# Last stage of a two-block kernel: row sums added up on VectorE, C rows multiplied as high and low parts, first half's last norm placed beside the second half's products

## The reference, cut to what matters

```python
u = ca * jax.nn.sigmoid(cg)
u = depthwise_conv(u, lp['c_conv'], C_CONV // 2, C_CONV // 2)      # 31 taps, 512 channels
u = layer_norm_2(u, lp['c_ln_g'], lp['c_ln_b'])                    # mean and variance over 512 channels
yc = jnp.einsum('btc,ce->bte', jax.nn.silu(u), lp['c_pw']) + lp['c_pw_b']
...
cat = jnp.concatenate([ya * jax.nn.silu(za), yb * jax.nn.silu(zb),
                       yc * jax.nn.silu(zc), yd * jax.nn.silu(zd)], axis=-1)   # 4 x 512 rows
y = jnp.einsum('bte,ed->btd', cat, lp['w_out'])
x = x + gate * y
return rms_norm_2(x, final_g)                                      # over 1024 channels
```

## Time and profile before

| | us |
|---|---|
| median of 3 runs | 3508.3 (3506.18 to 3508.97) |
| profiled execution, its own time | 3508.35 |
| its span in the trace | 3506.2 |
| TensorE busy in the span | 3327.1 (95%) |
| VectorE busy | 1903.7 (54%) |
| ScalarE busy | 1057.7 (30%) |

### The profile page before, as it was taken

The page is one execution under the profiler, slowest core; times in us unless marked ns, Lnnn a source line. Parts: engine busy times, 40 slices in busy tenths (PEclk is TensorE's granted clock), DMA queues, the critical chain, the costliest instruction groups (busy, mean ns, idle before and its releaser), DMA issues.

```text
span 3506.2 us, 37170 instructions
## 1 busy us (share of the span) xinstructions
PE 3327.1 (95%) x15356; PEld 2669.9 (76%) x15356; DVE 1903.7 (54%) x3141; ACT 1057.7 (30%) x1537; POOL 146.6 (4%) x72
## 2 busy tenths in 40 slices
PE   8999999999999999999999999999899899888997
PEld 7888888777888877777778888888676677667675
DVE  4323323267768688785543223223766877876443
ACT  3121121224332556562321111111543331322321
POOL 0000000000000000000000000000001033060000
PEclk9999999999999999999999999999999999999998
DMA  4211211112533420014111111111112111103131
GB/s 149 75 56 60 72 61 53 68 61 96 133 117 113 163 84 13 13 48 163 37 37 49 54 43 49 54 48 49 60 37 96 64 37 64 64 24 108 54 144 48
DMA packets 86808, 246.96 MB, mean 70 GB/s; under 512 B 8304, under 2 KB 22000, under 8 KB 85104
## 3 DMA queue, kind: packets, MB, share of 16 engines
q1 hardware_dynamic: 86640, 244.58, 20.2%
HBM read 200.51 MB, written 44.04 MB: 70 GB/s over the span
## 4 chain that ended last, share of the span: by engine, by line
PE 78%; DVE 15%; ACT 5%; issue 1%; DMA 1%; DVEq 0%; SPq 0%; ACTq 0%
PE PS L359 77%; DVE CV L1823 2%; PE PS L364 2%; DVE X L1823 1%; DVE WS L1815 1%; DVE XC L1823 1%; DVE HELD L1858 1%; DMA RAW<-in_W 1%; DVE XS L1823 1%; DVE RG L1823 1%; DVE GG L1815 1%; ACT RG L1045 1%; ACT WS L1045 1%; ACT PT L1045 1%; DVE TMP L1823 1%
## 5 line engine op out<-in xcount | busy, mean ns | idle before, releaser
L359 PE MATMUL PS<-XS,WS 128*128 128x512 f32 x8352 | 1964.1, 396 | 75.8 <-DVE TMP L1815 24.6
L359 PEld LDWEIGHTS PS<-XS,WS 128*128 128x128 f32 x8352 | 1584.1, 190 | 440.7 <-issue 90.4
L359 PE MATMUL PS<-HS,WS 128*128 128x512 f32 x2208 | 511.3, 392 | 8.7 <-DVE WS L1815 8.7
L359 PEld LDWEIGHTS PS<-HS,WS 128*128 128x128 f32 x2208 | 416.2, 189 | 98.7 <-issue 12.0
L1045 ACT ACTIVATE WS<-RAW 128x1024 fp32r<-128x1024 f32 x280 | 286.5, 1050 | 532.1 <-PE PS L359 428.8
L1815 DVE TENSOR_TENSOR TMP<-TMP,PS 128x512 f32<-128x512 f32 x112 | 76.5, 686 | 653.5 <-PE PS L359 645.1
L1815 DVE TENSOR_TENSOR WS<-RAW,WS 128x1024 fp32r<-128x1024 f32 x280 | 339.1, 1233 | 166.5 <-ACT WS L1045 166.1
L1045 ACT ACTIVATE TMP<-PS 128x512 f32<-128x512 f32 x184 | 108.9, 596 | 542.6 <-PE PS L359 475.5
L1823 DVE SCALAR_TENSOR_TENSOR X<-PS,X 128x512 f32<-128x512 f32 x160 | 110.1, 690 | 240.9 <-PE PS L359 240.4
L1045 ACT ACTIVATE HS<-TMP 128x512 fp32r<-128x512 f32 x88 | 55.6, 632 | 478.5 <-DVE TMP L1815 478.5
L1823 DVE SCALAR_TENSOR_TENSOR CV<-UU,COL,CV 128x1024 f32<-128x1024 f32 x120 | 163.6, 1363 | 3.6
(11 more groups left out here) (282 smaller groups left out, 3011.8 us busy)
## 6 DMA issues: line engine op xcount, KB each, us to landing
RAW<-in_W SPq DMA_DIRECT2D x286, 512.0 KB, 3.7
DC<-TMP SPq DMA_DIRECT2D x32, 256.0 KB, 4.2
X<-in_xT SPq DMA_DIRECT2D x8, 512.0 KB, 8.5
DX<-X SPq DMA_DIRECT2D x2, 2048.0 KB, 8.1
DCZ<-CA SPq DMA_DIRECT2D x8, 512.0 KB, 4.0
DGA<-TMP SPq DMA_DIRECT2D x16, 256.0 KB, 2.7
DGB<-TMP SPq DMA_DIRECT2D x16, 256.0 KB, 3.8
CZ<-DCZ SPq DMA_DIRECT2D x8, 512.0 KB, 6.1
```

The source lines that it names most:

```text
L359: done = d.matmul(out, l, r, start=first, stop=last)
```

## The change

All of it is in the last stage, apart from six additions on VectorE in the mixer stage ahead of it.

- **Row sums.** Where TensorE summed a row block at a time (four matmuls for a mean or a sum of squares over 512 channels, eight over 1024), VectorE now adds the blocks in `HELD` or `TMP` first and TensorE makes one matmul of the sum (two for the very last one, whose eighth block comes directly). The sum of the `CV` blocks is built in the mixer, behind each channel block's convolution.
- **Order of `c_norm`.** Both means stand behind P1; the sum of squares of half 0 behind P3 and of half 1 behind P5. On ScalarE the squares of half 0 stand in the first piece and those of half 1 in the fourth, ahead of half 0's root and SiLU.
- **C rows.** The two `c_pw` units become split units (the plan's kind changes from raw to split). ScalarE copies the normed rows to `CVH`, VectorE writes the rest to `CVL`, and `cp` takes 12 fp32r matmuls where it took 4 plain ones. SP loads one unit more ahead of the stores of the C rows.
- **Last norm.** The squares of half 0 are summed as its blocks finish; TensorE's sum stands behind the second product of half 1, and root, reciprocal and scalings of half 0 stand among VectorE's additions for half 1. The output leaves in eight DMAs of 2 blocks instead of four of 4.

```diff
@@ tensor, c_norm and outputs
             def mean(h):
...
-                e.wait_ge(ve("ones"), ve("cv", 3), *banks.free(use))
-                mms(group(bank(*use), [(ones[:], CV[:, k, half(h)]) for k in range(4)])).then_inc(*mm.inc(*use))
-
-            mean(0)
-            yield
-            square_sum("c", 0, 4, lambda k: tmp("sq", "c", 0, k))
-            mean(1)
-            yield
-            yield
-            square_sum("c", 1, 4, lambda k: tmp("sq", "c", 1, k))
-            yield
-            yield
+                e.wait_ge(ve("ones"), ve("cvs", 3, h), *banks.free(use))
+                mms([(bank(*use), ones[:], HELD[:, h, :], True, True)]).then_inc(*mm.inc(*use))
+
+            def squared(h):
+                use = ("sq", "c", h)
+                banks.take(use, (ve, "v", "c", h))
+                e.wait_ge(ve("cq", h, 3), *banks.free(use))
+                mms([(bank(*use), ones[:], tmp("sq", "c", h, 0), True, True)]).then_inc(*mm.inc("sq", "c", h, 3))
+
+            for h in range(2):
+                mean(h)
+            yield
+            for h in range(2):
+                yield
+                squared(h)
+                yield
...
-                        mms(group(bank(*use), [(raw(u, 512 * (m % 2) + 128 * k, 128), CV[:, k, half(h)])
-                                               for k in range(4)])).then_inc(*mm.inc(*use))
+                        product(u, 512 * (m % 2), 4, CVH, CVL, h, use, ac("csh", 1, 3), ve("csl", 1, 3))
...
-                    if h == 1:
-                        square(0, m)
-                        if m:
-                            square(1, m - 1)
-            square(1, 7)
+                    if h == 1 and m == 1:
+                        row_squares(0)
+            row_squares(1)
+
+        def row_squares(h):
+
+            use = ("sq", "out", h)
+            banks.take(use, (ve, "v", "out", h))
+            e.wait_ge(ve("sqs", 6 + (h == 0), h), *banks.free(use))
+            done = mms([(bank(*use), ones[:], HELD[:, h, :], True, h == 0)])
+            if h:
+                e.wait_ge(ac("sq", "out", 1, 7))
+                done = mms([(bank(*use), ones[:], tmp("sq", "out", 1, 7), False, True)])
+            done.then_inc(*mm.inc("sq", "out", h, 7))
@@ scalar, c_norm
+            def squared(h):
+                for k in range(4):
+                    use = ("sq", "c", h, k)
+                    tmps.take(use, (ve, "cq", h, k) if k else (mm, "sq", "c", h, 3))
+                    e.wait_ge(ve("cc", h, k), *tmps.free(use))
+                    act(tmp(*use), CV[:, k, half(h)], ACT.Square).then_inc(*ac.inc(*use))
+            def scaled(h):
                 root("c", h)
                 for k in range(4):
+                    x = CV[:, k, half(h)]
                     e.wait_ge(ve("cy", h, k))
-                    x = CV[:, k, half(h)]
                     act(x, x, ACT.Silu, bias=col("c_ln_b", k)).then_inc(*ac.inc("cs", h, k))
...
+                for k in range(4):
+                    e.wait_ge(ac("cs", h, k), ve("xs", "ab", 5, 0))
+                    act(CVH[:, k, half(h)], CV[:, k, half(h)], ACT.Copy).then_inc(*ac.inc("csh", h, k))
+
+            squared(0)
+            for _ in range(3):
+                yield
+            squared(1)
+            scaled(0)
+            for _ in range(2):
+                yield
+            scaled(1)
             yield
@@ scalar, outputs
             for m in range(8):
                 square(0, m)
-                if m:
-                    square(1, m - 1)
-            root("out", 0)
-            square(1, 7)
+            for m in range(8):
+                square(1, m)
+                if m == 2:
+                    root("out", 0)
             root("out", 1)
@@ vector, mixer and c_norm
                 convolve(31)
+                if ct:
+                    for h in range(2):
+                        s = HELD[:, h, :]
+                        e.wait_ge(ve("cv", ct), ve("cvs", ct - 1, h) if ct > 1 else ve("ln4", "y0", 7, h))
+                        tt(s, s if ct > 1 else CV[:, 0, half(h)], CV[:, ct, half(h)], ALU.add).then_inc(*ve.inc("cvs", ct, h))
...
+            def split(h):
+                for k in range(4):
+                    e.wait_ge(ac("csh", h, k))
+                    low(CVL[:, k, half(h)], CV[:, k, half(h)], CVH[:, k, half(h)]).then_inc(*ve.inc("csl", h, k))
+
+            for h in range(2):
+                mean(h)
+            yield
+            for h in range(2):
+                center(h)
+            yield
+            for h in range(2):
+                sum_squares(h)
+                yield
+                scale(h)
+                yield
+            for h in range(2):
+                split(h)
+                yield
@@ vector, outputs
+            for m in range(8):
+                gated_add(("co", m, 1))
+                add_square(1, m - 1)
+                if m == 2:
+                    rstd("out", 0, 1024, RMS_EPS, mm("sq", "out", 0, 7), HELD[:, 0, :])
+                if 2 < m < 7:
+                    for k in (2 * m - 6, 2 * m - 5):
+                        scale_out(0, k)
+            rstd("out", 1, 1024, RMS_EPS, mm("sq", "out", 1, 7), HELD[:, 1, :])
+            for k in range(8):
+                scale_out(1, k)
@@ sync
+        loads(277)
         for m in range(4):
             for h in range(2):
                 store_cat(8 + m, h, ve("cp", m, h))
             if m % 2:
-                loads(276 + m // 2)
+                loads(278 + m // 2)
@@ pack
-    w += [(np.concatenate([cpw[2 * j], cpw[2 * j + 1]], axis=1), "raw") for j in range(2)]
+    w += [(np.concatenate([cpw[2 * j], cpw[2 * j + 1]], axis=1), "split") for j in range(2)]
```

More of the change, by code:

```diff
@@ L242, in build @@
     CV = at("CV", 152, [128, 4, 1024], F32)
+    CVH, CVL = at("CVH", 168, [128, 4, 1024], F32R), at("CVL", 152, [128, 4, 1024], F32R)
     PB = at("PB", 168, [128, 1026], F32)
@@ L999, in outputs @@
             for h in range(2):
-                if h == 1:
-                    banks.resize(6)
                 for m in range(8):
@@ L1771, in square @@
                 use = ("sq", "out", h, k)
-                tmps.take(use, (mm, *use))
+                tmps.take(use, (mm, "sq", "out", 1, 7) if h and k == 7 else (ve, "sqs", max(k, 1), h))
                 e.wait_ge(ve("co", k, h), *tmps.free(use))
@@ L2781, in c_norm, with mean, center @@
         def c_norm():
-            def c_mean(h):
-                e.wait_ge(mm("cm", h), ve("ln4", "y0", 7, h))
+            def mean(h):
+                e.wait_ge(mm("cm", h))
                 ts(HELD[:, h, :], bank("cm", h), 1.0 / 512, None, ALU.mult).then_inc(*ve.inc("cm", h))
-            def c_center(h):
+            def center(h):
                 for k in range(4):
@@ L2790, in c_center, with sum_squares, scale @@
                     tt(x, x, HELD[:, h, :], ALU.subtract).then_inc(*ve.inc("cc", h, k))
-            def c_scale(h):
+            def sum_squares(h):
+                s = tmp("sq", "c", h, 0)
+                for k in range(1, 4):
+                    e.wait_ge(ac("sq", "c", h, 0), ac("sq", "c", h, k), *([ve("cq", h, k - 1)] if k > 1 else ()))
+                    tt(s, s, tmp("sq", "c", h, k), ALU.add).then_inc(*ve.inc("cq", h, k))
+            def scale(h):
                 e.wait_ge(ve("cc", h, 3))
@@ L2859, in outputs, with add_square, scale_out @@
                         low(XS[:, 1, k, :], XSf[:, 1, k, :], XS[:, 0, k, :]).then_inc(*ve.inc("cr", k))
-            for h in range(2):
-                for m in range(8):
-                    gated_add(("co", m, h))
-            for h in range(2):
-                e.wait_ge(ve("cy", h, 3))
-                rstd("out", h, 1024, RMS_EPS, mm("sq", "out", h, 7), HELD[:, h, :])
-                for k in range(8):
-                    x = X[:, k, half(h)]
-                    e.wait_ge(ve("rs", "out", h))
-                    stt(x, x, col("final_g", k), HELD[:, h, :], ALU.mult, ALU.mult).then_inc(*ve.inc("fin", k, h))
+            def add_square(h, k):
+                s, x = HELD[:, h, :], tmp("sq", "out", h, k)
+                if k == 1:
+                    e.wait_ge(ve("cy", h, 3), ac("sq", "out", h, 0), ac("sq", "out", h, 1))
+                    tt(s, tmp("sq", "out", h, 0), x, ALU.add).then_inc(*ve.inc("sqs", 1, h))
+                elif k > 1:
+                    e.wait_ge(ac("sq", "out", h, k), ve("sqs", k - 1, h))
+                    tt(s, s, x, ALU.add).then_inc(*ve.inc("sqs", k, h))
+            def scale_out(h, k):
+                x = X[:, k, half(h)]
+                e.wait_ge(ve("rs", "out", h), ac("sq", "out", h, k))
+                stt(x, x, col("final_g", k), HELD[:, h, :], ALU.mult, ALU.mult).then_inc(*ve.inc("fin", k, h))
+            for m in range(8):
+                gated_add(("co", m, 0))
+                add_square(0, m - 1)
+            add_square(0, 7)
+            for m in range(8):
+                gated_add(("co", m, 1))
[8 more added lines that the diff above has]
+                scale_out(1, k)
```

(6 more changed lines are left out.)

27 lines of the change are left out of this document (removed).

## The result

| | us |
|---|---|
| before, median of 4 runs beside it | 3508.03 (3506.18 to 3508.97) |
| with the change, median of 4 runs | 3488.89 (3485.69 to 3490.11) |
| ratio, with its 95% interval | 0.9941 (0.993 to 0.9953) |
| profiled execution: own time, span | 3490.11, 3487.2 |

A forecast was written before the change was run, and what follows sets the result against it. TensorE was taken as the bound from P1 to half 1's last product. Terms 0.2 - 5.7 - 10.6 - 3.8 = -19.9 on the 3506.2 us span gave 3486.3, with time outside the span 3488.4; range 3480 to 3494.

The forecast's parts named there:

- Mixer, 0: Mixer stage: six additions behind the convolutions fit in VectorE's idle time and cost 0.
- Start of the stage, +1.2: Last stage's start: splitting the first `c_pw` unit ahead of A and B rows delays 1.2 us, counted within `c_norm`.
- `c_norm`, +0.2: C norm: twelve matmuls go, but ScalarE's and VectorE's chain eats the gain; `cp` starts 0.2 us later in all.
- `cp`, -5.7: C rows' product: eight products take 2.72 us each instead of 3.43, 5.7 us less.
- Half 0 and `do`, 0: From `cp` to the end of half 0: later splits are ready in time and additions fit, 0.
- Half 1, -10.6: Half 1's products: 22.6 us from half 0's last pickup instead of 33.27, 10.6 us less.
- tail, -3.8: Last product to the end: 3.8 us less than 25.95, with VectorE late and two sums at half clock.
- (2): Rival in `c_norm`: TensorE keeps the pace, the chain being 6 to 9 us shorter; 3479 us, chance 0.12.
- (3): Rival in `c_norm`: the chain is longer through half clock, about 5 us more; 3493 us, chance 0.12.
- (4): Rival on ScalarE: each table switch on the path costs another 1.4 us; 3491.2 us, chance 0.05.
- (5): Rival at `do`: the D rows' load comes late; slower, 3512 us if 38 us later; chance 0.02.
- (6): Rival on the whole kernel: less than 7 us won; chance 0.02.

The follow-up runs named there:

- experiment 1: The kernel before with only the last norm's part of the change, C norm and C rows as before; 3494.15 us, ratio 0.9956.
- experiment 8: The changed kernel with reordered C norm, earlier last-norm root, scalings moved into the wait, and first `c_pw` unit split behind the A and B rows; 3472.89 us.
- experiment 5: The changed kernel with C norm sums of squares in `HELD` and the C norm's steps in another order, same work; 3478.93 us, ratio 0.9914.
- experiment 2: The changed kernel with the C rows' product as plain float32 again, no high and low parts; 3490.74 us, ratio 0.9944.
- experiment 4: The changed kernel with half 0's sum, root and reciprocal of the last norm one product earlier; 3484.53 us, ratio 0.9931.
- experiment 6: The changed kernel with half 0's last-norm root one product earlier and its last four scalings behind the last addition of squares; 3483.07 us.
- experiment 7: The changed kernel with 18 fp32r matmuls of unused result ahead of the last two sums; 3488.68 us, ratio 0.9942.
- experiment 3: The changed kernel with the C norm's squares added into `HELD` instead of a `TMP` slot; 3486.37 us, ratio 0.9933.

## Why the prediction was right

Where a time of the changed kernel is set against a forecast one or one of before, the 0.92 by which its stage began late is taken off; other times are as the profile has them.

- **Mixer, 0.** The six additions cost nothing that can be seen. The start of the stage moved by 0.92, of which 0.45 was there at the 56th microsecond of the program, ahead of anything that was changed. Over the stretch with the additions (before 2773.71 to 3189.73) it was 416.0 us before, 416.4 with the change, and 416.3 in experiment 1, which has no additions there.
- **Start of the stage, +1.2.** Measured 1.14 (wait for `XS` 4.12 against 2.98); experiment 8 removed it.
- **`c_norm`, +0.2.** `cp` starts 0.18 later than before (first pickups less one product: 3313.61 - 2.72 = 3310.89 against 3314.14 - 3.43 = 3310.71). The chain, step by step, forecast against measured: sum of half 0 picked up 3273.3, 3273.3; table load done 3276.4, 3276.3; SiLUs done 3284.0, 3283.9; high parts done 3286.4, 3285.95; additions done 3290.6, 3290.2; wait 6.4, 6.1; low parts done 3310.9, 3310.4. The price of the high parts was off: I took it from four squares in 2.44, and they took 2.17. But those squares were paced by VectorE's centring, 2.49 for four, and three squares with nothing in their way take 1.68 in the changed kernel (3274.26). So I had read a wait as a price. The step that was off most is P6 to P8, priced 16.3 + 2 to end at 3310.6: TensorE needed 19.16 us from the start of the sum to the end of P8 where I had 20.0, and ended at 3309.4. It did not show, since the low parts set the start of `cp`. They were done 0.5 early, and what made up for that is 0.14 from their end to `cp`'s first matmul, and the time between a product's end and its pickup, which the sum left out. So the mechanism was right, and that +0.2 came out to the tenth is luck. That the gain of twelve plain matmuls is eaten by this chain is what experiment 5 shows: with the chain reordered, all 9.3 appeared.
- **`cp`, -5.7.** Pickups at 3314.53 and 3317.25 are 2.72 apart, before 3.43. The size was right; experiment 2 shows that its net worth is 0.9, since the splits delay P1 and lengthen the `c_norm` chain. The forecast had both halves of this in different terms and did not set one against the other.
- **Half 0 and `do`, 0.** The last pickup of half 0 (3442.37) is 5.53 earlier than before where 5.5 was forecast. The D rows' high parts began at 3356.35, `do` at 3376.9: 20 us ahead.
- **Half 1, -10.6, and tail, -3.8.** The last product ended 16.2 earlier, where 16.1 was forecast. The tail is 22.2 us (forecast 22.15): reciprocal of half 0 done at 3457.26 (3457.3), last addition of squares 3468.78 (3469.1), sums 3472.6 (3472.55), last scaling 3482.8 (3482.7), end 3486.3 (3486.3). Times in brackets are the forecast's. Experiments 4, 6 and 7 show each of its two parts, the wait and the clock.

**The rivals.** TensorE did not keep the pace (2): 6.1 us of wait. The chain was not longer (3): the granted clock was 0.84 in the two us from 3294 on, 3 us into the work. No table load cost more (4): 3275.95 + 1.28 = 3277.23, and the root starts at 3277.24. The Trainium skill (ScalarE: Activation LUTs, What ACT_TABLE_LOAD costs) gives a drain of about 1380 ns for each switch. The trace does not show it: the load starts 0.01 us behind the last square and the root 0.01 behind the load. The D rows were not late (5). The gain was not below 7 us (6).

The remaining 0.9 between the forecast span of 3486.3 and the measured 3487.2 is the later start of this execution's stage, scatter that no term had. Outside the span this execution had 2.9 us where 2.15 was assumed. By the trace each term of the sum is right to 0.1 us, and each step on the chain of `c_norm` to half a microsecond, while P8, which was off the chain, ended 1.2 ahead of its forecast; the median's agreement within 0.5 is finer than the scatter of 4.4 us between its own runs allows one to claim.

## What to carry to other kernels

When work is taken off the engine that is the bound, follow the other engines in their new order before counting the gain: here the matmuls taken out of `c_norm` and `cp` were won only where the chain of square, sum, root, reciprocal, SiLU and split kept up, and 9.3 us came back by ordering that chain alone. Look at what stands between two steps of such a chain for another purpose (a weight unit's copy, scalings that nobody waits for, a slot whose release is a sum on another engine) and move it into a wait that is there anyway. And judge a change of a few microseconds by the length of its stage in the trace: the start of the stage wandered by 3.4 us between executions of kernels that are the same up to there.

## What was unexpected of the hardware

- **The price of a wait on TensorE is more than the wait.** The last two sums, two plain matmuls, took 3.81 us to the pickup behind a wait of 4.75, and 2.02 behind one of 0.67. In experiment 4 I expected that behind a wait of 2 the clock would be up; the wait was 3.29, and the first sum still took 1.67 and the second 1.91 us, at a granted clock of 0.50. Behind 1.44 they took 1.13 and 1.02.
- **What the clock costs behind a wait differs from one execution to the next.** P6 to P8, 72 matmuls that take 16.93 us at full clock in half 1, took 17.76 in experiment 6 and 18.06 in the changed kernel, both behind a wait of 6.10, and 19.12 in experiment 3 behind one of 3.79. So a longer wait did not mean a dearer return, and 0.8 to 2.2 us is as close as these traces give it.
- **A high part of 128x512 costs what a square costs.** Four copies to fp32r took 2.17 us and three squares 1.68, so each further one adds about 0.52 in either. The 2.44 for four squares is the pace of the centring that feeds them.
- **An output DMA of half the size lands in 2.8 us against 4.3**. From the end of the last scaling to the end it was 3.5, where I had 3.6; before, 4.9. The Trainium skill (DMA: Bandwidth & Descriptors, Anatomy of one DMA) gives a fixed part of about 2.0 us, fitted on DMAs that GpSimd issues, from which I had estimated 3.15 for the landing. These are issued by SyncE and landed in 2.8; a straight line through the two measured sizes would put the fixed part at 1.3, an estimate.
